# Carried heads of a stick-breaking attention layer score no tile in use 3: five score tiles and three value products take other places in the hand-written order

## The chip, the cores and the metric

One Trainium2 chip; the kernel runs on one of its cores. The metric is the device time of one execution in microseconds (us), lower is better. The engines are TensorE (PE, with PEld for its weight loads), VectorE (DVE), ScalarE (ACT), GpSimd (POOL) and SyncE (SP), which issues most of the DMAs.

## The reference, cut to what matters

Two layers over x of 1024 positions by 1024 features, float32: stick-breaking attention, then an HGRN2 recurrence. The change is in the first. For each of 8 heads of width 128:

```python
u = rms_norm(h, norm_gain)
q, k, v, gate = split(u @ w_in, 4)            # w_in: 1024 x 4096
q, k = rms_norm(q, q_gain), rms_norm(k, k_gain)
z = (q @ k.T) * 128 ** -0.5                   # strictly causal, s < t
log_skip_j = where(causal, log_sigmoid(-z), 0)
log_skip = reverse_cumsum(log_skip_j) - log_skip_j
weights = where(causal, exp(log_sigmoid(z) + log_skip), 0)
o = weights @ v
h = h + (o * silu(gate)) @ w_out
```

The reversed cumulative sum of logs is a product of sigmoids of -z over the positions to the right: the kernel forms it as a scan.

## The kernel before, in words

**Precision.** Every float32 product is made of three passes over parts: `matmul_exact` (L28 to L30) multiplies hi by hi, hi by lo and lo by hi. So each operand is split: ScalarE copies it into the rounded type (hi), VectorE subtracts (lo).

**A head in ten uses.** `build_attention` works in steps. In step h TensorE projects the inputs of head n = h + 1 and, between these projections, does the attention of head h. A step has ten uses of the projection banks: uses 0 to 7 make q, k and v of one tile of 128 positions each (24 matmuls with 384 columns), uses 8 and 9 make the gate for half the positions each (24 matmuls with 512 columns). In uses 3, 5, 7 and 9 q and k of two tiles are transposed as well (L1205, L1206, at kt = 5).

**The carried heads.** Heads 0 to 5 are "carried": their weights go through DRAM to be transposed. A head has eight tiles of query positions, and tile i has (i + 1) x 128 columns, the positions up to its own. They are taken in `ORDER = [4, 5, 6, 7, 2, 3, 0, 1]`; k below is the place in that order, so k = 0 is tile 4 and k = 3 is tile 7. For each k:

- "scores" on TensorE: three matmuls for each unit of up to 512 columns (L1223, L1225, L1227; tiles 4 to 7 have two units). On ScalarE: the sigmoids of -z into `skip` (L757) and of z into `beta` (L759), which wait until the `beta` buffer's last user (L990 of k - 3) is done. On VectorE: the scan (L940), the product with beta (L944) and the transposition in 32 x 32 blocks (L951).
- SP (`carry`) stores the transposed tile to DRAM (L611), waits for the landing, and reads two of its four quarters back (L574). "read" on ScalarE waits for the same landing and reads the other two. All four quarters land in `beta`, turned.
- "settle": ScalarE makes the hi part (`settle_weights`, L788), VectorE the lo part (`refine_weights`, L990). There are two slots for these, k % 2.
- "outputs" at = k // 2, the value product of a pair of tiles: TensorE multiplies v by the weights (L28 to L30 into `a_p_o`), after a wait for L990 of both tiles; then VectorE multiplies the gate by it (L1007). Pair 0 has 18 matmuls, pair 1 24, pair 2 12 and pair 3 6.

**The order.** It is written out by hand in the table `PLAIN` (L348 to L366), with one entry (what, head offset, k) for each piece. The same table drives all engines; each runs "before" ahead of its own part of the use, "mid" inside it and "after" behind it. On TensorE "mid" is at kt = 4 of 8 of the use's projection. On ScalarE and VectorE "before" is followed by the hi or lo copies of the transposed q and k, then "mid", then the copy and the squares of the projected tile (or the gate's sigmoid and product), then "after". Steps 0 to 5 use `PLAIN`; step -1 has an empty table; step 6 uses `SQUEEZED`, whose first entries still end the last carried head; step 7 uses `LAST`. A head offset of -1 means the head before.

**Other work in the same queues.** In uses 6 and 8 ScalarE and VectorE split the next input weights (1024 columns a piece). In steps 1 to 4 the attention also splits w_out into parts: SP loads half rows (`load_raw_half`), ScalarE and GpSimd split them in the uses of `SPLIT_AT`, SP stores the parts (`store_half`). SP runs `carry_all` in order: it waits for each tile's landing before it goes on, with the half rows and the store of the last head's output (at k = 5) between.

After the attention come its output projection, the recurrent layer and its output projection, which the change does not touch.

Of the kernel before, what the change touches and what calls it, by code (L numbers as in the profile page):

```python
# [324 lines left out]
def build_attention(nc, c, small_inputs, x, gain, stage, m_in, link, w_in, w_out, ut_hi, ut_lo,  # L325
# [8 lines left out]
    UNITS = ENDS[-1]  # L334
    ORDER = [4, 5, 6, 7, 2, 3, 0, 1]
    ORDER_ENDS = [sum(Z_UNITS[i] for i in ORDER[:k + 1]) for k in range(TILES)]
    NAT, GATE = TILES, 2

    def unit_blocks(i, u):

        if i == 4:
# [8 lines left out]
                        2: [("settle", 0, 0), ("scores", 0, 2)],  # L350
                        3: [("settle", 0, 1), ("scores", 0, 3)],
                        4: [("scores", 0, 4)],
                        5: [("settle", 0, 3), ("scores", 0, 5)],
                        6: [("scores", 0, 6)],
                        7: [("settle", 0, 4), ("scores", 0, 7)]},
             "mid": {0: [("outputs", -1, 3)],
                     1: [("read", 0, 0)],
                     2: [("read", 0, 1)],
                     3: [("read", 0, 2)],
                     4: [("read", 0, 3), ("outputs", 0, 0), ("settle", 0, 2)],  # L360
                     5: [("read", 0, 4)],
                     6: [("read", 0, 5)],
                     7: [("settle", 0, 5), ("read", 0, 6)],
                     8: [("read", 0, 7), ("outputs", 0, 2), ("settle", 0, 6)],
                     9: [("settle", 0, 7)]},
             "after": {6: [("outputs", 0, 1)]}}  # L366
    SQUEEZED = {"before": {0: [("scores", 0, 0), ("scores", 0, 1)],
# [8 lines left out]
                           9: [("mixed", 0, 0), ("mixed", 0, 1)]},  # L376
                "mid": {0: [("outputs", -1, 3)]},
                "after": {1: [("outputs", 0, 0)],
                          2: [("outputs", 0, 1)],
# [15 lines left out]
    GATE_EARLY = IN_ORDER[:6] + [("gate", 0), ("qkv", 6), ("qkv", 7), ("gate", 1)]  # L395
    SPLIT_AT = [5, 6, 8, 9]
    TURN_AT = 5
# [4 lines left out]
    with ExitStack() as ctx:  # L402
# [69 lines left out]
        wt_ready = sem("wt_ready")  # L472
# [120 lines left out]
        def _(sp):  # L593
# [22 lines left out]
            def carry_all(h, b):  # L616

                group = h - 1
                split = 0 <= group < 4
                if group >= 1:  # L620
                    store_half(sp, m_in, w_out, link, group - 1, 3)
                for k in range(TILES):
                    carry(h, k)
                    if k == 0 and group >= 1:
                        for i in range(2):
                            sp.wait_ge(link["w_parts_stored"][i], group * 64)
                    if k == 0 and split:
                        for i in range(2):
                            load_raw_half(sp, m_in, w_out, link, group, i)
                    if k == STORE_AT and h >= 1:  # L630
                        store(h - 1, 1 - b)
                    if k == 5 and split:
                        store_half(sp, m_in, w_out, link, group, 0)
                    if k == 6 and split:
                        store_half(sp, m_in, w_out, link, group, 1)
                        load_raw_half(sp, m_in, w_out, link, group, 2)
                    if k == 7 and split:
                        load_raw_half(sp, m_in, w_out, link, group, 3)
                        store_half(sp, m_in, w_out, link, group, 2)
# [52 lines left out]
        def _(act):  # L692
# [39 lines left out]
            def sigmoids(h, b, k):  # L732

                i = tile_of(h, k)
                for u in range(Z_UNITS[i]):
# [4 lines left out]
                    if u == 0:  # L740
                        act.wait_ge(rms_ready, TILES * h + i + 1)

                        if is_carried(h) or h == CARRIED and k < 2:
                            if k >= 2 or not known_first(h):
                                act.wait_ge(flip_stored[k % 2], 16 * (PAIRS * h + k // 2))
                            if not is_carried(h):
                                act.wait_ge(wt_ready, UNITS * h)
                            elif k >= 3:
# [869 lines left out]
def build_hgrn(nc, c, stage, m_in, link, w, w_in, w_out, ut_hi, ut_lo,  # L1618
# [10 lines left out]

    SPLIT_AT = [3, 4, 6, 7]  # L1630
    HALVES = SEQ // 2
# [851 lines left out]
```

## Time and profile before

| | us |
|---|---|
| median of 3 runs | 1162.79 |
| lowest and highest | 1162.35, 1163.99 |
| the profiled execution, its own time | 1163.26 |
| span of its instructions | 1161.4 |
| TensorE busy | 1143.8 (98% of the span) |
| VectorE busy | 823.9 (71%) |
| ScalarE busy | 415.8 (36%) |
| GpSimd busy | 171.6 (15%) |

How to read it: the span runs from the first to the last instruction, and the execution's time lies 1.9 us above it. TensorE's rows have modelled ends: consecutive matmuls overlap in them, so distances between starts say how long a piece took. A wait is listed as the engine's idle time before an instruction, with the instruction that released it.

### The profile page before, as it was taken

The numbers are of one execution on the slowest core, as the hardware profiler recorded it, in microseconds if no ns is written. First come the engines' busy times: TensorE is split into PE (matmuls) and PEld (weight loads), VectorE is DVE, ScalarE is ACT, GpSimd is POOL, SyncE is SP. The second block draws the span as 40 slices with busy tenths as digits, with TensorE's granted clock in tenths as the row PEclk, the third lists the DMA queues.
The fourth block names the chain that finished last, engine by engine and source line by source line (L and its number), as shares of the span: only waits on it lengthen the run. The fifth ranks groups of instructions, "written<-read, shape, count | busy, mean of one in ns | idle before, by whom it ended". The sixth has DMA issues, their size and how long they took to land. (4 is left out here: it accounts for less than half of the span.)

```text
span 1161.4 us, 19342 instructions
## 1 busy us (share of the span) xinstructions
PE 1143.8 (98%) x7012; PEld 1048.9 (90%) x7012; DVE 823.9 (71%) x1620; ACT 415.8 (36%) x887; POOL 171.6 (15%) x360
## 2 busy tenths in 40 slices
PE   8999999999999999999999999999999999999998
PEld 8999998989898989988888999999999999999787
DVE  5768776878677877674444787888888888788421
ACT  5544454444445444452223222323232322222200
POOL 2412133232333222110004000000000000000000
PEclk9999999999999999999999999999999999999999
DMA  8243447374645521165532112324232331118441
GB/s 253 56 120 107 132 139 211 117 213 130 216 140 177 161 83 47 60 265 179 177 100 82 37 38 56 100 72 134 85 120 91 110 93 35 47 37 310 140 141 73
DMA packets 145211, 141.76 MB, mean 122 GB/s; under 512 B 19936, under 2 KB 117472, under 8 KB 145120
## 3 DMA queue, kind: packets, MB, share of 16 engines
q1 hardware_dynamic: 106336, 120.88, 32.0%
q10 hardware_dynamic: 38784, 19.67, 6.4%
q8 instruction: 56, 0.92, 0.3%
q14 instruction: 35, 0.29, 0.1%
HBM read 93.86 MB, written 46.66 MB: 121 GB/s over the span
## 5 line engine op out<-in xcount | busy, mean ns | idle before, releaser
L28 PE MATMUL p_proj<-w_qkv_hi,ut_hi 128*128 128x384 f32 x504 | 172.8, 343 | 0.9 <-DVE a_gated L1015 0.6
L30 PE MATMUL p_proj<-w_qkv_hi,ut_lo 128*128 128x384 f32 x504 | 169.2, 336 | 0.0
L29 PE MATMUL p_proj<-w_qkv_lo,ut_hi 128*128 128x384 f32 x504 | 168.7, 335 | 0.0
L28 PE MATMUL p_proj<-w_ig_hi,next_hi 128*128 128x256 f32 x512 | 145.5, 284 | 0.0
L29 PE MATMUL p_proj<-w_ig_lo,next_hi 128*128 128x256 f32 x512 | 143.1, 279 | 0.0
L30 PE MATMUL p_proj<-w_ig_hi,next_lo 128*128 128x256 f32 x512 | 143.0, 279 | 0.0
L28 PE MATMUL p_proj<-next_hi,w_qf_hi 128*128 128x512 f32 x282 | 113.2, 401 | 0.0
L940 DVE TENSOR_TENSOR_SCAN a_skip<-a_skip,a_diagonal 128x641 f32<-128x641 f32 (+3 forms) x64 | 87.3, 1364 | 36.4 <-ACT a_beta L759 36.4
L30 PE MATMUL p_proj<-next_hi,w_qf_lo 128*128 128x512 f32 x282 | 110.1, 390 | 0.0
L29 PE MATMUL p_proj<-next_lo,w_qf_hi 128*128 128x512 f32 x282 | 109.9, 390 | 0.0
L28 PEld LDWEIGHTS p_proj<-w_qkv_hi,ut_hi 128*128 128x128 f32 x504 | 94.8, 188 | 2.2 <-DVE a_gated L1015 0.8
L28 PEld LDWEIGHTS p_proj<-w_ig_hi,next_hi 128*128 128x128 f32 x512 | 96.2, 188 | 0.0
L29 PEld LDWEIGHTS p_proj<-w_ig_lo,next_hi 128*128 128x128 f32 x512 | 96.2, 188 | 0.0
L30 PEld LDWEIGHTS p_proj<-w_ig_hi,next_lo 128*128 128x128 f32 x512 | 96.0, 188 | 0.0
L29 PEld LDWEIGHTS p_proj<-w_qkv_lo,ut_hi 128*128 128x128 f32 x504 | 94.9, 188 | 0.7
L30 PEld LDWEIGHTS p_proj<-w_qkv_hi,ut_lo 128*128 128x128 f32 x504 | 94.6, 188 | 0.0
L788 ACT ACTIVATE a_wt_hi<-a_beta 128x640 fp32r<-128x640 f32 (+7 forms) x48 | 33.0, 687 | 107.4 <-DMA flips_scratch<-a_skip 69.8
L2245 POOL TENSOR_TENSOR g_sum_eps<-g_sum_sq,head_eps 128x8 f32<-128x8 f32 x8 | 1.6, 200 | 429.3 <-ACT g_k_turned L1866 429.3
L849 ACT ACTIVATE a_raw<-p_proj 128x384 f32<-128x384 f32 x64 | 31.6, 494 | 93.1 <-PE p_proj L30 61.9
L30 PEld LDWEIGHTS p_proj<-next_hi,w_qf_lo 128*128 128x128 f32 x282 | 52.9, 188 | 11.6
L29 PEld LDWEIGHTS p_proj<-next_lo,w_qf_hi 128*128 128x128 f32 x282 | 53.1, 188 | 10.0
L28 PEld LDWEIGHTS p_proj<-next_hi,w_qf_hi 128*128 128x128 f32 x282 | 53.1, 188 | 9.9
(259 smaller groups left out, 2768.2 us busy)
## 6 DMA issues: line engine op xcount, KB each, us to landing
stage<-in_hg_w_in_dram SPq DMA_DIRECT2D x32, 512.0 KB, 4.3
stage<-in_sb_w_in_dram ACTq DMA_DIRECT2D x24, 512.0 KB, 5.4
w_out_hi_scratch<-m_in SPq DMA_DIRECT2D x32, 256.0 KB, 2.6
w_out_lo_scratch<-m_in SPq DMA_DIRECT2D x32, 256.0 KB, 2.8
m_in<-mixed_scratch SPq DMA_DIRECT2D x12, 448.0 KB, 5.8
a_gated<-in_x_dram SPq DMA_DIRECT2D x8, 512.0 KB, 4.0
m_in<-in_sb_w_out_dram SPq DMA_DIRECT2D x16, 256.0 KB, 4.1
ut_hi<-w_out_hi_scratch SPq DMA_DIRECT2D x8, 512.0 KB, 8.1
```

Source lines behind the costliest of these rows:

```text
L28: pe.matmul(out, w_hi, m_hi, start=start, stop=False, skip_group_check=True)
L29: pe.matmul(out, w_hi, m_lo, start=False, stop=False, skip_group_check=True)
L30: return pe.matmul(out, w_lo, m_hi, start=False, stop=stop, skip_group_check=True)
L788: act.activation(slot_of(wt_hi, h, k), flipped_blocks(h, k), ACT.Copy).then_inc(wt_hi_ready, Z_UNITS[tile_of(h, k)])
L849: act.activation(raw[t % 4][:, :, :], p_proj[i % 2][:, 0:3, :], ACT.Copy).then_inc(raw_ready, 1)
L940: dve.tensor_tensor_scan(chain, chain, diagonal[:, SEQ - width:SEQ + 1][:, ::-1], 0.0, ALU.mult, ALU.add).then_inc(scan_done, 1)
L2245: pool.tensor_tensor(sum_eps[:, :], sum_sq[:, :], c["head_eps"][:, :], ALU.add).then_inc(rms_ready, 1)
```

## The change

It edits the table `PLAIN` and what hangs on it, and adds and removes no computation.

- No tile is scored before use 3. The scores of tiles 7, 2, 3, 0, 1 (k = 3 to 7), which stood before uses 3 to 7, stand before uses 4 to 8.
- The value products: pair 0 (tiles 4 and 5) from mid use 4 to behind use 3; pair 1 (tiles 6 and 7) stays behind use 6; pair 2 (tiles 2 and 3) from mid to behind use 8; pair 3 (tiles 0 and 1) from mid to behind use 0 of the next step.
- The reads of k = 3 to 7 by ScalarE stand one or two uses later (mid 5 to 9). The settling of k = 3 goes from before use 5 to before use 6, of k = 5 from mid 7 to mid 8, of k = 6 from mid 8 to mid 9, of k = 7 from mid 9 to mid 0 of the next step; k = 0, 1, 2 and 4 are settled where they were.
- `SQUEEZED` takes the last carried head's settling and product in the same way, and the first sigmoids of head 6 wait for L990 up to k = 6 of head 5, not k = 7.
- The half rows of w_out are split in uses 4, 5, 8, 9, not 5, 6, 8, 9, and SP issues their stores and loads behind k = 4, 5, 6 where it did behind 5, 6, 7.

```diff
--- before.py
+++ after.py
@@ -348,22 +348,26 @@
     PLAIN = {"before": {0: [("scores", 0, 0)],
                         1: [("scores", 0, 1)],
                         2: [("settle", 0, 0), ("scores", 0, 2)],
-                        3: [("settle", 0, 1), ("scores", 0, 3)],
-                        4: [("scores", 0, 4)],
-                        5: [("settle", 0, 3), ("scores", 0, 5)],
-                        6: [("scores", 0, 6)],
-                        7: [("settle", 0, 4), ("scores", 0, 7)]},
-             "mid": {0: [("outputs", -1, 3)],
+                        3: [("settle", 0, 1)],
+                        4: [("scores", 0, 3)],
+                        5: [("scores", 0, 4)],
+                        6: [("settle", 0, 3), ("scores", 0, 5)],
+                        7: [("settle", 0, 4), ("scores", 0, 6)],
+                        8: [("scores", 0, 7)]},
+             "mid": {0: [("settle", -1, 7)],
                      1: [("read", 0, 0)],
                      2: [("read", 0, 1)],
                      3: [("read", 0, 2)],
-                     4: [("read", 0, 3), ("outputs", 0, 0), ("settle", 0, 2)],
-                     5: [("read", 0, 4)],
-                     6: [("read", 0, 5)],
-                     7: [("settle", 0, 5), ("read", 0, 6)],
-                     8: [("read", 0, 7), ("outputs", 0, 2), ("settle", 0, 6)],
-                     9: [("settle", 0, 7)]},
-             "after": {6: [("outputs", 0, 1)]}}
+                     4: [("settle", 0, 2)],
+                     5: [("read", 0, 3)],
+                     6: [("read", 0, 4)],
+                     7: [("read", 0, 5)],
+                     8: [("settle", 0, 5), ("read", 0, 6)],
+                     9: [("settle", 0, 6), ("read", 0, 7)]},
+             "after": {0: [("outputs", -1, 3)],
+                       3: [("outputs", 0, 0)],
+                       6: [("outputs", 0, 1)],
+                       8: [("outputs", 0, 2)]}}
     SQUEEZED = {"before": {0: [("scores", 0, 0), ("scores", 0, 1)],
                            1: [("turn", 0, 0), ("turn", 0, 1), ("scores", 0, 2), ("scores", 0, 3)],
                            2: [("turn", 0, 2), ("turn", 0, 3), ("scores", 0, 4)],
@@ -374,8 +378,9 @@
                            7: [("scores", 1, 2), ("turn", 1, 0), ("outputs", 0, 3), ("turn", 1, 1), ("scores", 1, 3)],
                            8: [("turn", 1, 2), ("turn", 1, 3), ("scores", 1, 4), ("scores", 1, 5)],
                            9: [("mixed", 0, 0), ("mixed", 0, 1)]},
-                "mid": {0: [("outputs", -1, 3)]},
-                "after": {1: [("outputs", 0, 0)],
+                "mid": {0: [("settle", -1, 7)]},
+                "after": {0: [("outputs", -1, 3)],
+                          1: [("outputs", 0, 0)],
                           2: [("outputs", 0, 1)],
                           3: [("turn", 0, 4)],
                           4: [("turn", 0, 5)],
@@ -393,7 +398,7 @@
 
     IN_ORDER = [("qkv", i) for i in range(NAT)] + [("gate", half) for half in range(GATE)]
     GATE_EARLY = IN_ORDER[:6] + [("gate", 0), ("qkv", 6), ("qkv", 7), ("gate", 1)]
-    SPLIT_AT = [5, 6, 8, 9]
+    SPLIT_AT = [4, 5, 8, 9]
     TURN_AT = 5
     STORE_AT = 5
     QUARTER = P // 4
@@ -629,13 +634,14 @@
                             load_raw_half(sp, m_in, w_out, link, group, i)
                     if k == STORE_AT and h >= 1:
                         store(h - 1, 1 - b)
+                    if k == 4 and split:
+                        store_half(sp, m_in, w_out, link, group, 0)
                     if k == 5 and split:
-                        store_half(sp, m_in, w_out, link, group, 0)
-                    if k == 6 and split:
                         store_half(sp, m_in, w_out, link, group, 1)
                         load_raw_half(sp, m_in, w_out, link, group, 2)
+                    if k == 6 and split:
+                        load_raw_half(sp, m_in, w_out, link, group, 3)
                     if k == 7 and split:
-                        load_raw_half(sp, m_in, w_out, link, group, 3)
                         store_half(sp, m_in, w_out, link, group, 2)
 
             def store(h, b):
@@ -744,7 +750,7 @@
                             if k >= 2 or not known_first(h):
                                 act.wait_ge(flip_stored[k % 2], 16 * (PAIRS * h + k // 2))
                             if not is_carried(h):
-                                act.wait_ge(wt_ready, UNITS * h)
+                                act.wait_ge(wt_ready, UNITS * (h - 1) + ORDER_ENDS[6])
                             elif k >= 3:
                                 act.wait_ge(wt_ready, UNITS * h + ORDER_ENDS[k - 3])
                             elif not known_first(h):
```

## Rows read from the trace of the kernel before

**Rows 1.** The page: TensorE's busy time and the granted clock in 40 slices of the span.
```profile
PE 1143.8 (98%) x7012; PEld 1048.9 (90%) x7012; DVE 823.9 (71%) x1620; ACT 415.8 (36%) x887; POOL 171.6 (15%) x360
...
PEclk9999999999999999999999999999999999999999
```

**Rows 2.** Who waited for whom, TensorE: us in total, times, longest.
```profile
PE a_p_o L28 <- DVE a_wt_lo L990: 7.1, 6, 1.7
...
PE p_proj L28 <- DVE a_gated L1015: 0.6, 1, 0.6
```

**Rows 3.** Timeline, TensorE, fourth carried head: start us, duration us, instruction, [idle before].
```profile
248.80 0.34 PE L1223 MATMUL p_pair<-a_kt_hi,a_qt_hi 128*128 128x384 f32 x1
...
249.70 0.34 PE L28 MATMUL p_proj<-w_qkv_hi,ut_hi 128*128 128x384 f32 x1
...
254.59 0.39 PE L1223 MATMUL a_p_z<-a_kt_hi,a_qt_hi 128*128 128x512 f32 x1
...
255.64 0.34 PE L28 MATMUL p_proj<-w_qkv_hi,ut_hi 128*128 128x384 f32 x1
...
259.81 0.39 PE L1223 MATMUL p_pair<-a_kt_hi,a_qt_hi 128*128 128x512 f32 x1
...
265.19 0.39 PE L1223 MATMUL p_pair<-a_kt_hi,a_qt_hi 128*128 128x512 f32 x1
...
266.58 0.34 PE L28 MATMUL p_proj<-w_qkv_hi,ut_hi 128*128 128x384 f32 x1
...
271.21 0.34 PE L1223 MATMUL a_p_z<-a_kt_hi,a_qt_hi 128*128 128x384 f32 x1
...
271.74 0.34 PE L28 MATMUL p_proj<-w_qkv_hi,ut_hi 128*128 128x384 f32 x1
...
278.06 0.39 PE L1223 MATMUL p_pair<-a_kt_hi,a_qt_hi 128*128 128x512 f32 x1
...
278.76 0.34 PE L28 MATMUL p_proj<-w_qkv_hi,ut_hi 128*128 128x384 f32 x1
...
300.45 0.39 PE L28 MATMUL a_p_o<-a_wt_hi,a_v_hi 128*128 128x256 f32 x1 [1.67 <-DVE a_wt_lo L990]
```

**Rows 4.** Timeline, VectorE and ScalarE around the head's first use.
```profile
250.08 0.41 DVE L990 TENSOR_TENSOR a_wt_lo<-a_beta,a_wt_hi 128x256 fp32r<-128x256 f32 x1
...
250.36 0.57 ACT L757 ACTIVATE a_skip<-p_pair,a_inv_rms 128x384 f32<-128x384 f32 x1
...
254.55 0.85 DVE L951 STREAM_TRANSPOSE a_skip<-a_beta 128x640 f32<-128x640 f32 x1
```

**Rows 5.** Timeline: tile 5's L990 here; its scores and L990 two heads earlier.
```profile
270.87 0.97 DVE L990 TENSOR_TENSOR a_wt_lo<-a_beta,a_wt_hi 128x768 fp32r<-128x768 f32 x1
...
131.59 0.39 PE L1223 MATMUL a_p_z<-a_kt_hi,a_qt_hi 128*128 128x512 f32 x1
...
146.08 0.97 DVE L990 TENSOR_TENSOR a_wt_lo<-a_beta,a_wt_hi 128x768 fp32r<-128x768 f32 x1
```

**Rows 6.** Timeline: a sigmoid released by scores (tile 5), then tile 7's chain.
```profile
255.49 0.69 ACT L757 ACTIVATE a_skip<-a_p_z,a_inv_rms 128x512 f32<-128x512 f32 x1 [0.20 <-PE a_p_z L1227]
...
270.30 0.67 ACT L757 ACTIVATE a_skip<-p_pair,a_inv_rms 128x512 f32<-128x512 f32 x1
...
272.74 2.29 DVE L940 TENSOR_TENSOR_SCAN a_skip<-a_skip,a_diagonal 128x1025 f32<-128x1025 f32 x1 [0.90 <-ACT a_beta L759]
...
276.32 1.25 DVE L951 STREAM_TRANSPOSE a_skip<-a_beta 128x1024 f32<-128x1024 f32 x1
...
284.40 1.06 ACT L788 ACTIVATE a_wt_hi<-a_beta 128x1024 fp32r<-128x1024 f32 x1 [1.87 <-issue]
...
285.56 1.23 DVE L990 TENSOR_TENSOR a_wt_lo<-a_beta,a_wt_hi 128x1024 fp32r<-128x1024 f32 x1 [1.20 <-ACT a_wt_hi L788]
```

**Rows 7.** DMA issues of the page: KB each, median us from issue to landing.
```profile
stage<-in_hg_w_in_dram SPq DMA_DIRECT2D x32, 512.0 KB, 4.3
...
w_out_hi_scratch<-m_in SPq DMA_DIRECT2D x32, 256.0 KB, 2.6
```

## The prediction

> **What bounds the kernel now.** I read the page first. TensorE is busy for 1143.8 of 1161.4 us, and the slices of the whole span show it at 9 tenths: only 17.6 us of it stand idle, and its clock is granted in full [rows 1]. So an edit that leaves its matmuls as they are can win at most part of those 17.6 us, and it loses whatever new time TensorE stands. Next I read the list of waits, for TensorE alone [rows 2]. Its largest entry is the one that this change touches: six times, once in each carried head, a value product stands for the fine part of the weights that VectorE makes at L990, 7.1 us in all and 1.7 at most. The timeline shows which one: the product of pair 2 (tiles 2 and 3) in the middle of use 8 (start 300.45 [rows 3]). One wait of 0.6 us for a gate product is there too [rows 2]. A gap is shown short by about 0.17 us: 24 projection matmuls take 4.17 us from start to start, 0.17 each, while each row is 0.34 long [rows 3]. So the stands removed can be worth 7.1 + 0.6 + 7 x 0.17 = **8.9 us**.
>
> After that I read, in the head that starts at 248.80, how far apart TensorE's milestones lie, and how long each tile needs from the start of its scores to the end of its L990. Both are needed, since all three products move relative to the scores that feed them. I write S for the start of the scores named.
>
> **Distances on TensorE** [rows 3]: scores of tile 4, 0.90 (248.80 to 249.70); a plain qkv use, 4.17 (255.64 to 259.81); a qkv use with a turn in it, 4.63 (266.58 to 271.21); scores of tile 7, 1.39 (265.19 to 266.58); of tile 2, 0.53; of tile 3, 0.70.
>
> **Part 1: the last product (tiles 0 and 1) moves from mid use 0 to behind use 0, and its settling from mid use 9 to mid use 0 of the next head.** VectorE used to do this L990 in use 9 (250.08, 0.41 us [rows 4]; TensorE was by then at the next head's scores). Now it stands in "mid" of use 0, and on VectorE "before" comes first: scan, product and transposition of the new head's tile 4. The transposition ended at 254.55 + 0.85 = 255.40, S + 6.60 [rows 4]. With 0.41 and a handover of 0.03 the fine weights are there at S + 7.04. TensorE reaches the product at S + 0.90 + 4.17 = 5.07. **A new stand of 2.0 us**, in the five heads that follow a carried head in this plan. In the squeezed plan the new head's first two tiles are 128 and 256 wide and are not transposed, so I cost it at nothing there. Lower bound: ScalarE began the first sigmoid at S + 1.56 (250.36), for tile 5 it began at S + 0.90 (255.49 [rows 6]); with all of that gone, 1.3 us. Upper: one more 0.6 us activation ahead of it, 2.6. Five times 2.0 is **+10.0** (6.5 to 13).
>
> **Part 2: the first product (tiles 4 and 5) moves from mid use 4 to behind use 3.** From the start of tile 5's scores TensorE now comes to it after 10.60 (254.59 to 265.19, uses 1 and 2 with their scores) and 4.63 (use 3, no scores now): 15.23. The fine weights of tile 5 ended at 271.84 [rows 5], that is 17.25 after the 254.59. In the head that starts near 126 they took 146.08 + 0.97 - 131.59 = 15.46 [rows 5]. So the stand is 2.0 us in the one and 0.2 in the other. Nothing in tile 5's own chain moves. But the stand of part 1 lies between tiles 4 and 5, so tile 4's work is out of its way sooner, and the w_out loads that SP issues between them have more time. I take 0.8, below the middle of the two, for each of six heads: **+4.8** (0 to 12).
>
> **Part 3: tile 7's scores go from use 3 to use 4, the pair's product stays behind use 6.** TensorE's distance from tile 7's scores to the product is 1.39 + 4.17 + 0.53 + 4.63 + 0.70 + 4.17 = 15.6; the first product, two turns of order and use 3 used to lie in it as well. The chain on the other side, each step without a queue ahead of it [rows 6]: first sigmoid at S + 0.90; four sigmoids, 2.44 (270.30 to 272.74); scan to the end of the transposition, 4.83 (272.74 to 277.57); store and quarter reads through DRAM until ScalarE starts to settle, 6.83 (277.57 to 284.40); settling and L990, 2.39 (to 286.79). Sum 17.4. **A stand of 1.8 us in six heads, +10.8.** Before, the chain took 21.6 (265.19 to 286.79), because ScalarE and VectorE first had tile 5 to settle; the empty use 3 takes that 4.2 away, but the distance shrinks by more. Bounds: the 6.83 are two transfers of 512 KB behind each other. The nearest DMA rows are 2.6 us for 256 KB and 4.3 for 512 KB [rows 7]: twice the one gives a stand of 0.2, twice the other 3.6. I take the chain's own rows, since it is the same tile on the same queues. By the Trainium skill ("DMA: Bandwidth & Descriptors", section "Anatomy of one DMA", a fit for another issue path), a transfer costs some 2.0 us fixed plus its bytes at 436 GB/s; two of 512 KB would be 6.4 us by that, an estimate, the stand 1.4 and the sum 2.6 lower. The trace has the duration, and it goes ahead.
>
> **Part 4: the product of tiles 2 and 3 moves from mid to behind use 8, its tiles one use later.** In the old order 15.0 us lay between the end of tile 7's settling (285.46) and the release of this product (300.45). In the new one TensorE spends from there: 1.3 until the pair-1 product starts, some 2.8 for it (24 matmuls of 256 columns, estimated from 4.17 for 384), 4.63 for use 7, about 0.8 for two small scores and 5.6 for the gate use (estimated at 512 columns): 15.1. ScalarE also no longer stands for tile 2's L990 before the last tile's sigmoids. So the old stand goes, and I cost the new one at nothing; if that cover fails it is at most the 1.7 us of today, in six heads.
>
> **Parts without a price.** SP's half-row stores and loads are issued one step of k earlier, behind their tile's reads; they are the same transfers, and queue for nothing that TensorE needs in use 4 to 7. ScalarE and GpSimd split the halves in uses 4 and 5, where both have idle time while tile 7 is in VectorE. The looser wait of the squeezed head's first sigmoids only takes one L990 out of it, and it must, or it would hold the head up. The p_o bank and the weight slots come free as before: each settling follows the product two places earlier.
>
> **Sum** for the profiled execution: 1163.26 - 8.9 + 10.0 + 4.8 + 10.8 = 1180.0 us. It stands 0.47 above the median of the runs shown, so the forecast of the median is **1179.5 us**. About 0.2% is what a measurement of this kernel can tell from no change, 2.3 us.
>
> **The rivals.**
> (a) The transfers shrink to the short rows. With 2.6 us a leg pair 1 stands 0.2 us and pair 0 not at all; part 1 has no transfer in it and stays. 1162.8 + 10.0 + 1.2 - 8.9 = 1165. For: the stores have fewer neighbours. Against: tile 7's round trip had hardly any neighbour before either. Chance 0.10.
> (b) Faster: the chains contract wherever ScalarE and VectorE come free. All three new stands are differences of 2 us between times of 7 to 17; if queueing that I count as work falls out of each, by 2 us, nothing stands and 8.9 are won: 1154. It decides once the new stands together fall under 8.9, a third of my 25.6. For: tile 7's chain loses 4.2 that way. Against: part 1 is scan, product and transposition in a row on one engine. Chance 0.04.
> (c) Use 8 becomes a new stand. ScalarE reads tile 0 back in the middle of use 8, once its store has landed, and SP issues that store behind the head's output and a half row. While ScalarE waits, the splitting of the next qkv weights, the gate's sigmoid and VectorE's gate product wait behind it, and TensorE needs these for the next head (the 0.6 of today [rows 2] is this). 1.5 us in six heads: 1188.5. Chance 0.12.
> (d) TensorE's clock falls. Today's stands of up to 1.7 us leave the granted clock full [rows 1], and the new ones are 2 us. Were each of 17 new stands followed by one projection use at 1.2 in place of 2.4 GHz, that is 4.17 us each, 71 in all, about 1251. Chance 0.02. The Trainium skill ("TensorE: Matmul & The Clock Gate", section "HAM oscillation") warns of just this pattern, bursts that start cold after every idle gap; by that rule, the trace before agrees only in that its short gaps cost no clock.
> (e) The move does nothing measurable: stands of 1.5 us come in place of those of 1.5. Then 1163; this needs my three sums to be a third in size. Chance 0.02.
> The forecast's own case has 0.70.
>
> **The numbers.** Range 1169 to 1188: its ends take part 1 at its bounds (-3.5, +3), part 3 at a stand of 1.0 or 2.3 (-5, +3), and part 2 from 0.2 to 1.5 (-3.5, +4), not all on one side. It leaves out most of (a), (b), (d) and (e) and half of (c). Faster by over 0.2%: (b) and a little of (a), 0.05. Within 0.2%: 0.02. Slower: 0.93.
>
> **What would show it.** TensorE's waits on L990 grow from 7.1 to about 23 us, 17 in place of 6, in three places for each head: behind use 0 (2.0), behind use 3 (about 1) and behind use 6 (1.8); none at the product behind use 8. Behind use 0 VectorE's transposition of tile 4 ends right before the L990 that releases it. ScalarE does not stand for L990 before the last tile's sigmoids. TensorE's busy time stays at 1144 us. The forecast is wrong if one of the places has no stand, or if VectorE does the tile-1 L990 before the new head's scan.

## The result, and the profile after

| | us |
|---|---|
| before, median of 4 runs beside it | 1162.57 (1161.83 to 1163.99) |
| after, median of 4 runs | 1201.13 (1199.39 to 1201.99) |
| ratio, 95% interval | 1.0326 [1.0314, 1.0339] |
| span of the profiled execution, before and after | 1161.4, 1199.3 |

Slower by 38.6 us, where 17 were forecast: the direction is right, the size is not, and the range up to 1188 does not hold it. The granted clock is 0.984 on average in each of the four executions of after and 0.999 in the profiled one of before, so the lower clock belongs to the kernel and not to one execution.

The page of the kernel after, TensorE's busy time and granted clock, which answer to [rows 1]:

```profile
PE 1160.4 (97%) x7012; PEld 1063.8 (89%) x7012; DVE 823.5 (69%) x1620; ACT 420.7 (35%) x887; POOL 166.4 (14%) x360
...
PEclk9999998999999999999999999999999999999999
```

The same 7012 matmuls take 16.6 us longer (1160.4 against 1143.8). In the page the clock hardly shows; only one slice of 40 falls to 8. The list of waits of the kernel after (total, times, longest; L996 is L990 of before) answers to [rows 2]:

```profile
PE a_p_o L28 <- DVE a_wt_lo L996: 29.3, 11, 4.2
```

Stands on the fine weights grow from 7.1 to 29.3 us, 22.2 more. With the 16.6 that is 38.8; less the 0.6 us wait for the gate product, which is gone, it is 38.2, and the span grew by 37.9. So there are two causes, in the proportion of four to three: TensorE stands longer, and its matmuls themselves run slower. (As in the prediction, the list shows each stand some 0.17 us short; the stands forecast as 25.6 would read 25.6 - 17 x 0.17 = 22.7 in it.) Both lie in the attention, as two stretches show, first of the kernel before and then of the one after (window in us, length, busy time of PE, PEld, DVE, ACT, POOL with instructions, granted clock, share of the DMA engines, GB/s):

```profile
60.00:469.00 409.00, 400.58 (x2352) 379.08 (x2351) 307.00 (x650) 194.90 (x385) 110.38 (x228) 1.00 0.47 141
```

```profile
60.00:507.00 447.00, 417.32 (x2353) 394.19 (x2352) 306.87 (x650) 200.12 (x386) 105.10 (x228) 0.96 0.43 129
...
268.90:272.10 3.20, 0.00 (x0) 0.00 (x0) 3.13 (x4) 0.48 (x1) 0.00 (x0) 1.00 0.91 280
272.80:276.20 3.40, 3.40 (x14) 3.11 (x13) 1.36 (x7) 1.53 (x4) 1.43 (x4) 0.50 0.35 113
276.20:279.60 3.40, 3.40 (x21) 3.40 (x20) 2.83 (x3) 0.46 (x2) 0.00 (x0) 1.00 0.74 226
```

The same work takes 447 us where it took 409; what comes behind it takes 692.4 us before and 692.3 after. The last three rows are one stand and what follows: TensorE idle for 3.2 us, then 14 matmuls at a granted clock of 0.50, which is 1.2 GHz, then 21 in the same length at 2.4 GHz. There are nine such half-rate stretches, each at or behind a stand; the two at the stands of 4.25 and 3.06 us are twice as long as the others. The eleven stands, in the timeline of the kernel after (start, duration, instruction, idle before it and its releaser):

```profile
105.74 0.39 PE L28 MATMUL a_p_o<-a_wt_hi,a_v_hi 128*128 128x256 f32 x1 [1.77 <-DVE a_wt_lo L996]
...
134.54 0.39 PE L28 MATMUL a_p_o<-a_wt_hi,a_v_hi 128*128 128x256 f32 x1 [2.47 <-DVE a_wt_lo L996]
...
170.58 0.58 PE L28 MATMUL a_p_o<-a_wt_hi,a_v_hi 128*128 128x256 f32 x1 [2.12 <-DVE a_wt_lo L996]
...
202.56 0.58 PE L28 MATMUL a_p_o<-a_wt_hi,a_v_hi 128*128 128x256 f32 x1 [4.25 <-DVE a_wt_lo L996]
...
241.01 0.39 PE L28 MATMUL a_p_o<-a_wt_hi,a_v_hi 128*128 128x256 f32 x1 [2.07 <-DVE a_wt_lo L996]
...
272.19 0.39 PE L28 MATMUL a_p_o<-a_wt_hi,a_v_hi 128*128 128x256 f32 x1 [3.33 <-DVE a_wt_lo L996]
...
309.65 0.39 PE L28 MATMUL a_p_o<-a_wt_hi,a_v_hi 128*128 128x256 f32 x1 [1.98 <-DVE a_wt_lo L996]
...
340.62 0.39 PE L28 MATMUL a_p_o<-a_wt_hi,a_v_hi 128*128 128x256 f32 x1 [3.13 <-DVE a_wt_lo L996]
...
378.18 0.39 PE L28 MATMUL a_p_o<-a_wt_hi,a_v_hi 128*128 128x256 f32 x1 [2.07 <-DVE a_wt_lo L996]
...
409.11 0.42 PE L28 MATMUL a_p_o<-a_wt_hi,a_v_hi 128*128 128x256 f32 x1 [3.08 <-DVE a_wt_lo L996]
...
447.65 0.58 PE L28 MATMUL a_p_o<-a_wt_hi,a_v_hi 128*128 128x256 f32 x1 [3.06 <-DVE a_wt_lo L996]
```

They alternate between two places. The first, third, and so on are pair 1's, behind use 6: 13.1 us in six (forecast 10.8, which would read 9.8 here). The others are pair 3's, behind use 0: 16.3 in five (forecast 10.0, which would read 9.2). Pair 0 has no entry in the list and idles 0.1 us in one head (forecast 4.8 in six), pair 2 stands nowhere (forecast nothing). All but the first two of the eleven have a half-rate stretch behind them.

Why pair 3's are 3.3 us and not 2.0 shows in the timeline of the kernel after around one of them, TensorE, ScalarE and VectorE together (ACTq is ScalarE issuing DMAs):

```profile
262.70 2.97 ACTq L246 DMA_DIRECT2D stage<-in_sb_w_in_dram  x3
...
263.61 0.34 PE L1229 MATMUL p_pair<-a_kt_hi,a_qt_hi 128*128 128x384 f32 x1
...
265.77 0.60 ACT L819 ACTIVATE a_gated<-p_proj 128x512 f32<-128x512 f32 x1 [3.09 <-issue]
...
266.79 0.57 ACT L763 ACTIVATE a_skip<-p_pair,a_inv_rms 128x384 f32<-128x384 f32 x1
...
270.98 0.84 DVE L957 STREAM_TRANSPOSE a_skip<-a_beta 128x640 f32<-128x640 f32 x1
271.75 0.38 DVE L996 TENSOR_TENSOR a_wt_lo<-a_beta,a_wt_hi 128x256 fp32r<-128x256 f32 x1
```

VectorE does what was forecast: tile 4's transposition, then at once the L996 that TensorE waits for. But the first sigmoid of tile 4 starts at S + 3.2, not at S + 1.56 [rows 4]. ScalarE reads tile 1 back at the end of use 9 now, a use later than before; behind that it issues three loads of input weights, 2.97 us in which it computes nothing, then the gate's sigmoid, and only then the sigmoids of the new head. TensorE ends use 9 at 263.8, so of the 2.97 us some 2.0 delay the gate's sigmoid. In the same head the kernel before issues the three loads one at a time, between ScalarE's other work, and each takes about 0.4 us (247.02, 247.74 and 248.87). The last of them there, and the longest block of three in after:

```profile
248.87 0.37 ACTq L246 DMA_DIRECT2D stage<-in_sb_w_in_dram  x1
```

```profile
192.16 3.89 ACTq L246 DMA_DIRECT2D stage<-in_sb_w_in_dram  x3
```

The blocks of three in the five heads take 2.72, 3.89, 2.97, 2.77 and 2.71 us, and the stands behind them are 2.47, 4.25, 3.33, 3.13 and 3.08: the longest block comes ahead of the longest stand.

### The profile page after: what moved, and what is told of

It is laid out like the page before. It is cut to its first block and busy times, and to the rows that moved or that the text cites. A ratio compares the mean times of both kernels' runs of the same rounds, so it can differ in the third digit from the quotient of the medians.

```text
span 1199.3 us, 19342 instructions
## 1 busy us (share of the span) xinstructions
PE 1160.4 (97%) x7012; PEld 1063.8 (89%) x7012; DVE 823.5 (69%) x1620; ACT 420.7 (35%) x887; POOL 166.4 (14%) x360
## 3 DMA queue, kind: packets, MB, share of 16 engines
q1 hardware_dynamic: 106336, 120.88, 31.2%
## 5 line engine op out<-in xcount | busy, mean ns | idle before, releaser
L28 PE MATMUL a_p_o<-a_wt_hi,a_v_hi 128*128 128x256 f32 (+1 forms) x160 | 49.2, 307 | 29.8 <-DVE a_wt_lo L996 29.3
L28 PEld LDWEIGHTS a_p_o<-a_wt_hi,a_v_hi 128*128 128x128 f32 x160 | 34.6, 216 | 34.8 <-DVE a_wt_lo L996 33.5
```

What stands on the lines that cost most here:

```text
L28: pe.matmul(out, w_hi, m_hi, start=start, stop=False, skip_group_check=True)
```

## The experiments

Each is timed against the kernel before, on the same chip (its medians lay between 1162.75 and 1163.27). "Waits" are TensorE's on the fine weights (L990 to L996 in the various kernels): us, times, longest.

### e1: the same order, the stands filled

Ahead of its wait TensorE transposes the identity 16 times at pair 1 and 22 times at pair 3, into a bank that the product then overwrites.

```diff
+                if at == 1 and is_carried(h):
+                    keep_running(16)
+                if at == 3 and h < CARRIED - 1:
+                    keep_running(22)
                 pe.wait_ge(wt_ready, UNITS * h + units_to(h, 2 * at + 1))
```

> The changed kernel with TensorE kept running while it would stand: 16 transpositions of the identity ahead of the pair-1 product's wait for L996 and 22 ahead of the pair-3 product's, in the carried heads, into the bank that the product then overwrites. The product waits for the same weights. Theory A (the stands cost 21.6 us and the clock that falls behind them another 16.6): the granted clock stays full, the matmuls lose nothing, and the time falls from 1201 to about 1184, though the stands' time is still there, as transpositions. Rival B (the clock falls for another reason, such as load or the new order itself): the clock still shows half rate in the same places and the time stays at 1201 or rises. A half result, 1190 to 1195, would mean that filling only part of a stand does not hold the clock.

Measured: 1190.26 us, ratio 1.0241 [1.0224, 1.0258], against 1201.13 for after. Page, list of waits and the stretch behind the stand of pair 3 in the same head:

```profile
PE 1168.3 (98%) x7218; PEld 1072.8 (90%) x7218; DVE 823.3 (69%) x1620; ACT 421.2 (35%) x887; POOL 166.2 (14%) x360
```

```profile
PE a_p_o L28 <- DVE a_wt_lo L996: 9.2, 10, 1.8
```

```profile
271.60:275.00 3.40, 3.40 (x23) 3.27 (x22) 1.63 (x8) 2.00 (x4) 1.43 (x4) 1.00 0.54 166
```

206 more matmuls, at 0.107 us each, are 22.0 us. The rest of TensorE's busy time is 1146.3, 14.1 under after and 2.5 over before. Fill and stands together are 31.2, no less than the 29.3 of after. So the chain is as late as it was, and the 10.9 us won are the clock's: 23 matmuls at full rate where after had 14 at half. One half-rate stretch of the nine is left, behind a stand of 1.80 us (mean clock 0.998). The time lies above the 1184 of Theory A, in what was called a half result: besides this stretch, 2.5 us more go into fill, stands and other gaps than stood idle in after.

### e2: part 1 taken back to front

Tile 1 is settled before the new head's tile 4 is scored, its product stays behind use 0.

```diff
-    PLAIN = {"before": {0: [("scores", 0, 0)],
+    PLAIN = {"before": {0: [("settle", -1, 7), ("scores", 0, 0)],
...
-             "mid": {0: [("settle", -1, 7)],
-                     1: [("read", 0, 0)],
+             "mid": {1: [("read", 0, 0)],
```

> The changed kernel with the settling of the last tile (k = 7) of the head before put ahead of the new head's first scores (before use 0, not mid use 0; the same in the squeezed head). Theory A (the stand behind use 0 is there because VectorE scans and transposes tile 4 before the L996 that the product waits for): these stands of 2.5 to 4.3 us vanish (16 us in five heads), and with them the half-rate stretches behind them (about 8 us): 1177. Rival B (the weights of k = 7 land too late in any case): the stand stays at 2 us or more and the first scores' sigmoids wait too: 1195 or more. The pair-1 stands of 2 us stay.

Measured: 1187.92 us, 1.0220 [1.0202, 1.0237].

```profile
PE a_p_o L28 <- DVE a_wt_lo L995: 23.5, 13, 3.8
```

That is 11 us above Theory A. Pair 3's five stands are gone but for one of 0.27, pair 1's are there as before (1.8 to 2.2 each). New ones stand at pair 0, behind use 3: 0.24, 1.04, 1.81, 2.35, 3.79 and 2.21 us, 11.4 in all. So part 1's mechanism is right: VectorE's order inside use 0 made the stand. And it had hidden part 2's.

### e3: the product of pair 1 in mid use 7

```diff
-                     7: [("read", 0, 5)],
+                     7: [("outputs", 0, 1), ("read", 0, 5)],
...
-                       6: [("outputs", 0, 1)],
```

> The changed kernel with the pair-1 product moved from behind use 6 to the middle of use 7 (some 2.4 us later on TensorE). Theory A (tile 7's chain of 17.4 us is longer than the 15.6 that TensorE leaves it): the six stands there (13 us) vanish, with the half-rate stretches behind them (about 10 us): 1178 if nothing else moves. Rival B: the settling of tile 2 waits for this product, so tiles 2, 3, 0 and 1 come later, a stand of 1 to 3 us appears behind use 8, and more at the product of pair 3: 1190 or more.

Measured: 1185.05 us, 1.0186 [1.0169, 1.0203], above the 1178 of Theory A; the stand that rival B puts behind use 8 does not come.

```profile
PE a_p_o L28 <- DVE a_wt_lo L995: 18.6, 8, 3.9
PE p_proj L28 <- DVE a_gated L1020: 2.4, 4, 1.2
```

Half a use more in front of the product ends pair 1's stands (0.89 in the last head). Pair 3 still stands 2.9 to 3.9, and four stands for the gate's product have come. I put these down to ScalarE's and VectorE's work of use 7, which now comes later; that is read from the order, not shown by a run. The profiled span fell by 13.6: 10.7 less on the fine weights, 5.4 less of TensorE's busy time (1155.0), 2.4 more at the gate product.

### e4: e2 and e3 together

> Both of these edits in one kernel. Theory A: all new stands and all half-rate stretches are gone, and the stands of the kernel before (8.9 us) do not come back: 1155 to 1165, at or under the kernel before at 1162.6. Rival B of the run with the pair-1 product later: stands behind use 8 instead, with the clock falling behind them, 1170 or more.

Measured: 1182.12 us, 1.0171 [1.0154, 1.0188], far above the 1155 to 1165 of Theory A, and with no stand behind use 8, where rival B had it. The two gains, 13.2 and 16.1, do not add; together they are 19.0.

```profile
PE a_p_o L28 <- DVE a_wt_lo L994: 16.2, 6, 5.2
PE p_proj L28 <- DVE a_gated L1019: 2.9, 4, 0.9
```

All six are now pair 0's: 0.22, 1.29, 2.82, 5.19, 4.12 and 2.51. That is part 2 of the forecast with nothing left to hide it, and over its upper bound of 12.

### e5: the three loads out of the chain of use 0

ScalarE issues the loads of use 9 behind its part of the next use 0.

```diff
-                    if plan is PLAIN and i == USES - 1 and not (isinstance(h, int) and h == HEADS - 3):
-                        for p in range(3):
-                            load(h + 3, p)
...
+                    if plan is PLAIN and i == 0 and not known_first(h):
+                        for p in range(3):
+                            load(h + 2, p)
```

> The changed kernel with ScalarE's three loads of the next input weights issued behind its work of use 0, not ahead of the gate's sigmoid of use 9. Theory A (of the stands behind use 0, 3.1 to 4.3 us where 2.0 was forecast, the rest is ScalarE issuing DMAs while TensorE has ended use 9, so that the new head's first sigmoids start 3 us behind their scores, not 1.6): the stands shrink to about 2.0 us (6 us less in all), the sigmoid of tile 4 begins 1.5 to 2 us behind the start of its scores, and some of the half-rate stretches go: 1188 to 1195. Rival B (the issues fit into time in which ScalarE waits anyway, or the later loads hold up the splitting in use 8): the stands stay over 3 us or come back elsewhere: 1199 or more.

Measured: 1201.48 us, 1.0314 [1.0292, 1.0337], no change to after. The list of waits, then the timeline (SPq is SP's queue):

```profile
PE a_p_o L28 <- DVE a_wt_lo L996: 33.2, 17, 3.5
```

```profile
267.62 0.57 ACT L763 ACTIVATE a_skip<-p_pair,a_inv_rms 128x384 f32<-128x384 f32 x1
...
272.69 0.33 SPq L616 DMA_DIRECT2D flips_scratch<-a_skip  x1
...
273.02 0.39 PE L28 MATMUL a_p_o<-a_wt_hi,a_v_hi 128*128 128x256 f32 x1 [1.38 <-DVE a_wt_lo L996]
...
280.13 0.80 SPq L579 DMA_DIRECT2D a_beta<-flips_scratch  x2
...
292.66 0.58 PE L28 MATMUL a_p_o<-a_wt_hi,a_v_hi 128*128 128x256 f32 x1 [3.46 <-DVE a_wt_lo L996]
```

The reading of the three issues is right: without them the first sigmoid of tile 4 starts 1.21 us behind its scores (267.62; scores at 266.41), and pair 3 stands 0.89 to 1.72, below the 2.0 of the forecast. But tile 4's store, issued at 272.69, is read back only 7.4 us later, with the loads in flight beside it, and pair 0 now stands 1.90 to 3.47 in five heads. The gain of one place was lost at the next, as rival B had it. In after, from which e5 differs in nothing but the place of the loads, the store of the same tile in the same head is issued at 271.85 and read back from 274.18 on, 2.3 us later; over the five heads that follow a carried one it is 2.2 to 4.0 us in after and 5.2 to 7.4 in e5. So moving the loads slows the store's return; by which step of the transfer is not shown.

### e6 and e7: pair 0 back in mid use 4

e6 is e4 with this, e7 is e6 with the loads of e5:

```diff
-                     4: [("settle", 0, 2)],
+                     4: [("outputs", 0, 0), ("settle", 0, 2)],
...
-                       3: [("outputs", 0, 0)],
```

> The kernel with the last tile settled first and pair 1 in mid use 7, and pair 0 moved back from behind use 3 to mid use 4, where it stood before the change. In the run without this the stands had gathered at pair 0 (1.3 to 5.2 us, 16 us in all, with 20 us at half rate behind them). Theory A (each product stands where tile chains and distance differ; with 3.5 us more for pair 0 the last stands go): the stands on L994 fall under 5 us, the clock stays full but for one or two stretches, 1160 to 1168. Rival B (the lateness comes from ScalarE and VectorE being behind at the start of a head and only moves on to the next product): stands of 2 us or more at pairs 1 and 2, 1172 or more.

> The same with the three loads of input weights issued behind use 0 too. Theory A (ScalarE is late at the start of a head because it issues them ahead of the gate's sigmoid): the gate product's stands (2.9 us in four) shrink under 1, and the time is 2 to 4 us below the run without this edit, 1157 to 1165, at the kernel before or under it. Rival B: no difference, within 1 us of it.

Measured: e6 1169.39 us, 1.0057 [1.0039, 1.0075]; e7 1180.09 us, 1.0145 [1.0128, 1.0162]. The lists of waits, e6 and then e7:

```profile
PE a_p_o L28 <- DVE a_wt_lo L993: 9.1, 7, 2.2
...
PE p_proj L28 <- DVE a_gated L1018: 1.5, 4, 0.7
```

```profile
PE a_p_o L28 <- DVE a_wt_lo L993: 15.8, 11, 2.1
```

With part 2 undone, 12.7 us of e4's time go. What stands in e6 is pair 1 again (0.43 to 2.16, five times), which e4 had hidden, and TensorE's busy time is 1144.6 us at a clock of 1.000. So with no tile in use 3, but the products and the settling where their chains allow it, 6.1 us of the 38.6 are left, 9.1 us of stands where Theory A had under 5. Three of them, of 1.86, 2.06 and 2.16 us, have no half-rate stretch behind them. e7 is 10.7 slower than e6, which neither theory had: the gate's stands do shrink (0.7 us in two), but the loads do more harm in use 0 than in use 9.

### b1: part 1 alone, put into the kernel before

```diff
-             "mid": {0: [("outputs", -1, 3)],
+             "mid": {0: [("settle", -1, 7)],
...
-                     9: [("settle", 0, 7)]},
...
+             "after": {0: [("outputs", -1, 3)],
+                       6: [("outputs", 0, 1)]}}
```

> The kernel before with one part of the change alone: the settling of the last tile in mid use 0 of the next head, its product behind use 0, and the looser wait of the squeezed head; all scores and all other products stand where they were. Theory A (VectorE's order alone makes a stand of 2 us there, as forecast; the rest of the measured 3 to 4 comes with the later reads): 2.0 us in five heads, +10, while the stands of 7.1 us at pair 2 stay; with a clock that falls behind some of them, 1173 to 1183. Rival B (the stand is as long as in the changed kernel, since it hangs on the scan and not on ScalarE's lateness): 3 us or more in each, 1180 or more.

Measured: 1169.78 us, 1.0048 [1.0031, 1.0065].

```profile
PE a_p_o L28 <- DVE a_wt_lo L991: 11.4, 8, 2.4
```

Five stands behind use 0: 1.31, 1.96, 1.81, 2.42 and 1.62, in all 9.1 where the forecast's 10.0 would read 9.2. Here the read of tile 1 is still in use 8 and the sigmoids come when they came. The old stands at pair 2 shrank from 7.1 to 2.3, so the product's later place gives some slack to the rest. The time lies below the 1173 of Theory A, mainly for these 4.8 us. TensorE's busy time is 1145.9, 2.1 more than before, with two half-rate stretches, behind the stands of 1.96 and 1.81; behind the longest, 2.42, there is none. The step holds by itself; what it got wrong is that the change also moves ScalarE's read, with the loads behind it, into its chain.

### b2 and b3: longer stands in the old order, without and with fill

These ask whether the clock falls for the new order or for the length of a stand. b2 is the kernel before with pair 2's product moved ahead of use 8; b3 adds 30 transpositions of the identity ahead of its wait.

```diff
                         7: [("settle", 0, 4), ("scores", 0, 7)]},
+                        8: [("outputs", 0, 2)]},
...
-                     8: [("read", 0, 7), ("outputs", 0, 2), ("settle", 0, 6)],
+                     8: [("read", 0, 7), ("settle", 0, 6)],
```

> The kernel before with one thing moved: the product of pair 2 from mid use 8 to before use 8, 2.7 us earlier on TensorE, so that its six stands of 1.1 us on average should be some 3.8 us long (16 us more). All scores and settlings stand where they were. Theory A (the clock falls behind a stand that is long enough, whatever the order around it): half-rate stretches appear behind most of these stands in a kernel that had none, and the time rises by more than the stands, 1185 to 1195. Rival B (the half-rate stretches belong to the new order): the clock stays full and the time rises by the stands alone, 1176 to 1180.

> The same with 30 transpositions of the identity (3.2 us) ahead of that product's wait. Theory A: the clock stays full and the time is the stands alone, 1176 to 1180, so that the difference to the run without them is the price of the clock. Rival B: no difference between the two, or this one is slower.

Measured: b2 1186.61 us, 1.0210 [1.0195, 1.0226]; b3 1178.31 us, 1.0138 [1.0116, 1.0160]. Waits, page and the stretch behind one stand of b2:

```profile
PE a_p_o L28 <- DVE a_wt_lo L991: 21.7, 6, 5.0
```

```profile
PE 1153.0 (97%) x7012; PEld 1058.0 (89%) x7012; DVE 824.7 (70%) x1620; ACT 416.9 (35%) x887; POOL 169.3 (14%) x360
```

```profile
311.90:315.30 3.40, 3.40 (x14) 3.30 (x15) 1.30 (x7) 0.00 (x0) 1.43 (x4) 0.50 0.99 313
```

and of b3 waits and page:

```profile
PE a_p_o L28 <- DVE a_wt_lo L991: 2.9, 4, 0.8
```

```profile
PE 1163.4 (99%) x7192; PEld 1069.2 (91%) x7192; DVE 825.0 (70%) x1620; ACT 417.1 (35%) x887; POOL 175.9 (15%) x360
```

In the old order too, a half-rate stretch follows each of the six stands of 2.6 to 5.0 us, and TensorE's busy time rises by 9.2. With the stands filled the mean clock is 1.000, busy time without the fill (180 x 0.107 = 19.3) is 1144.1, and 8.3 us are won although fill and the stands left (19.3 + 2.9, and 2.0 for VectorE's use of the bank, which the fill now waits for) are no less than the 21.7. Both times are as Theory A had them. The clock follows TensorE's standing idle.

How long a stand has to be is only partly settled. In the fourteen traces of this study, all 25 stands of 2.51 us or more on VectorE's fine weights or gate product have a half-rate stretch at them, and none under 1.77 has one. Of the 34 between 1.77 and 2.47 us, 18 have one and 16 have not.

### b4 and b5: part 4 alone, and with ScalarE's read moved too

b4 puts pair 2's product behind use 8 in the kernel before; b5 puts the product and tile 1's read ahead of use 9.

```diff
-                     8: [("read", 0, 7), ("outputs", 0, 2), ("settle", 0, 6)],
-                     9: [("settle", 0, 7)]},
+                     8: [("read", 0, 7)],
+                     9: [("settle", 0, 6), ("settle", 0, 7)]},
...
-             "after": {6: [("outputs", 0, 1)]}}
+             "after": {6: [("outputs", 0, 1)],
+                       8: [("outputs", 0, 2)]}}
```

```diff
                         7: [("settle", 0, 4), ("scores", 0, 7)]},
+                        9: [("outputs", 0, 2), ("read", 0, 7)]},
...
-                     8: [("read", 0, 7), ("outputs", 0, 2), ("settle", 0, 6)],
-                     9: [("settle", 0, 7)]},
+                     9: [("settle", 0, 6), ("settle", 0, 7)]},
```

> The kernel before with part 4 alone: the product of pair 2 behind use 8, and the settling of tile 0 in mid use 9 (not mid use 8), since it waits for that product. Everything else as before. Theory A (the product only comes 2.7 us too early, and the rest of the change is not needed for it): the six stands of 7.1 us go, no other comes, and it is faster than the kernel before by 5 to 9 us: 1154 to 1158. Rival B (settling tiles 0 and 1 late holds up ScalarE and the gate product of use 9, or pair 3 in the next head): 1160 or more.

> The kernel before with the product of pair 2 behind use 8 (written as before use 9), tile 0 settled in mid use 9, and ScalarE's read of the last tile (k = 7) before use 9, not in mid use 8. In the run without the last edit the stands at pair 2 were gone, but 5.5 us of stands at the gate's product had come, and ScalarE stood 6.9 us in use 8 for the landing of that tile's store. Theory A (these gate stands come from this one read): they go, the clock stays full, 1153 to 1158, ratio to the kernel before under 0.996. Rival B (the tile then lands too late to be settled in mid use 9, and ScalarE is late with the second gate half): stands of 1 us or more at the gate product or at pair 3, 1160 or more.

Measured: b4 1162.38 us, 0.9998 [0.9988, 1.0008]; b5 **1157.26 us, 0.9952 [0.9938, 0.9965]**. List of waits and a row of ScalarE's timeline in b4, then the waits of b5:

```profile
PE p_proj L28 <- DVE a_gated L1016: 5.5, 4, 2.1
```

```profile
243.15 1.06 ACT L700 ACTIVATE w_qkv_hi<-stage 128x1024 fp32r<-128x1024 f32 x1 [6.88 <-DMA flips_scratch<-a_skip]
```

```profile
PE p_proj L28 <- DVE w_gate_lo L898: 1.7, 2, 0.9
...
PE a_p_o L28 <- DVE a_wt_lo L990: 0.7, 1, 0.7
```

b4 takes the 7.1 us of stands at pair 2 away and gets 5.5 at the gate product for them. ScalarE stands 6.88 us in the middle of use 8, until the last tile's store has landed, and the weights' splitting and the gate's sigmoid wait behind it. It stood as long there in the kernel before:

```profile
243.98 0.31 ACT L788 ACTIVATE a_wt_hi<-a_beta 128x128 fp32r<-128x128 f32 x1 [6.85 <-DMA flips_scratch<-a_skip]
```

I read this so: there TensorE stood at pair 2 first and came to the gate product late enough; without that stand it comes too early for it. Once the read follows the product into use 9 (b5), both stands are gone, and the kernel is faster than the one before and the one after.

## Why the prediction was wrong in its size

**What bounds the kernel.** Right: TensorE, and the wait on L990 is what the edit moves. But the new time that TensorE stands is not all that such an edit can lose, as the next point shows. The 8.9 us of stands removed is at best an upper bound: b5 wins 5.6 (0.48% of 1162.8).

**The clock, rival (d).** This is the step that failed: the sum has no term for the clock. I carried "stands of up to 1.7 us leave the granted clock full" [rows 1] over to stands taken as 2.0, gave the other case 0.02, and said that busy time would stay at 1144. It rose by 16.6, by far the larger part of the 21.6 us missing. e1, b2 and b3 show the cause: the clock falls to half behind stands, and stays full when they are filled. The price in the rival was too high: 17 stands at 4.17 each, 71 us, where nine stretches cost 16.6 / 9 = 1.8 each in after, and 9.2 / 6 = 1.5 in b2. The Trainium skill ("TensorE: Matmul & The Clock Gate", section "HAM oscillation — how this bites in real kernels") warned of bursts that start cold after idle gaps; the traces agree, with 14 matmuls where 21 to 23 fit. The gaps that the Trainium skill warns of there are longer than most of these stands. Here stands of 1.8 to 2.5 us did it in about half of the cases, and for this kernel that measurement decides.

**Part 1, +10.0.** The mechanism is shown (e2 takes it away, b1 gives 9.1 alone). The term was mis-sized: 16.3, over its upper bound of 13. The first sigmoid "at S + 1.56" came from a head in which ScalarE had read tile 1 back a use earlier and issued its loads one at a time. I did not follow ScalarE's read into use 9, with the loads and the sigmoid behind it. Without the loads (e5) each stand is 1.4 to 2.9 us shorter.

**Part 2, +4.8.** Measured 0.1, and for the reason given only in part. Tile 4's work was out of tile 5's way, as stated. But the half-rate stretch behind the stand also lengthened TensorE's way to the product. The timeline of after: tile 5's scores, its L996 and the pair's product:

```profile
273.04 0.73 PE L1229 MATMUL a_p_z<-a_kt_hi,a_qt_hi 128*128 128x512 f32 x1
...
288.43 0.97 DVE L996 TENSOR_TENSOR a_wt_lo<-a_beta,a_wt_hi 128x768 fp32r<-128x768 f32 x1
...
289.77 0.28 PE L28 MATMUL a_p_o<-a_wt_hi,a_v_hi 128*128 128x256 f32 x1
```

The way is 16.73 us long, not 15.23, and L996 ends at 289.40, 0.37 before the product. The chain itself took 16.36 in this head, inside the 15.46 to 17.25 of the forecast; with the way as forecast there would have been a stand of about 1.1 (an estimate from these figures). With part 1's stand gone, these stands come (11.4 in e2, 16.2 in e4). My four terms were not independent, and adding them up was an error of its own. That the total of both, 16.3 + 0.1, is near 10.0 + 4.8 confirms neither: the one was too small and the other too large.

**Part 3, +10.8.** Measured 13.1, where the forecast would read 9.8: 2.2 us a stand, within the bounds of 0.2 to 3.6. The place is shown by e3. Rival (a), legs of 2.6 us, is out.

**Part 4, nothing.** Right: no stand at pair 2, and none in b4, which has this part alone. Rival (c) had a true mechanism, as b4 shows, but not in this change, where the last tile's read moves to use 9 as well: in after ScalarE waits for the landing of a store six times, 1.9 to 2.5 us each, and never in uses 8 and 9. There the moved read cost time in another way, by the loads behind it in part 1.

**Against the sum.** Stands alone: 29.3 as the list shows them, for a forecast that would read 22.7. With the clock left as it was the time would have been near 1163 + 22 = 1185, inside the range; this is an estimate. e1, where the clock was nearly full, took 1190.3, with the fill that replaced the stands a little longer than they were.

**Left open.** What decides between 1.77 and 2.47 us: in after no half-rate stretch follows the stands of 1.77 and 2.47, while 1.98 has one. Why three loads in a row hold ScalarE for 2.7 to 3.9 us and single ones for 0.4. And how the 7.4 us of the store in e5 divide between the weights' loads and the w_out traffic.

## What to carry to other kernels

For each consumer that an edit moves, compare its producer's chain and the bounding engine's distance from the same start, and go through what that chain's engines issue in the same place, DMA issues too: a read of returned data should move along with its consumer. Stands on such a loop are coupled, so one that is removed uncovers the next; sum them as a sequence, not as separate terms. Where TensorE is 98% busy as here, price each new stand of 2.5 us or more at its length plus 1.5 to 1.8 us for the clock (the means of b2 and after), give one of 1.8 to 2.5 us about half the chance of that, and look for it as busy time that has grown with the same number of matmuls.

## What the hardware showed that I had not expected

- Single stands of 2 to 4 us, some 30 us apart, are enough for the granted clock to drop to 0.50 behind them: nine stretches in after behind eleven stands, six behind six in b2. Fill by transpositions of 0.107 us held it at 1.000 (b3) and 0.998 (e1), and won 8.3 and 10.9 us with no result any earlier.
- Issuing three loads in a row held ScalarE for 2.97 us (262.70 in after; 2.71 to 3.89 in the five heads), longer than the sigmoids of a tile of 640 columns that waited behind them. Issued one at a time, in the same head of before, a load took about 0.4.
- A store of 320 KB with loads in flight beside it took 7.4 us from issue to the reading back (e5). With the loads issued in use 9 instead it took 2.3 (after, same tile and head).
